# Expert rows added to h in memory by an accumulating scatter for each block, in the mixture-of-experts tail of a hybrid decoder step

## The reference, cut to what matters

```python
h = h + concat([attn_out, ssd_out]) @ w_out
h = h + hier_moe(rmsnorm(h, norm2_w), ...)      # top 2 of 8 experts inside the top 1 of 4 groups
y = rmsnorm(h, norm_f_w)

# hier_moe -> grouped_experts: each (token, k) pair goes to a slot of its expert,
# blocks of rows belong to one expert
hdn = silu(xb @ w_gate[e]) * (xb @ w_up[e])      # 1024 -> 512
yr = hdn @ w_down[e]                             # 512 -> 1024
out = zeros.at[row_tok].add(yr * row_w[:, None]) # row_w is the gate of that pair
```

## Time and profile before

| | us |
|---|---|
| median of 3 runs | 3809.22 |
| the profiled execution, its own time | 3812.94 |
| its span, first to last instruction | 3811.1 |
| all stages ahead of mix_out end at about | 2277.9 |
| last slot made (L2573) | 2640.6 |
| experts' first instruction | 2688.46 |
| first transpose of gathered rows | 2707.26 |
| last copy of an expert result ends | 3674.08 |
| first gather of combine | 3679.63 |

### The profile page before, as it was taken

The page is one execution under the profiler, slowest core; times in us unless marked ns, Lnnn a source line. Parts: engine busy times, 40 slices in busy tenths (PEclk is TensorE's granted clock), DMA queues, the critical chain, the costliest instruction groups (busy, mean ns, idle before and its releaser), DMA issues. The chain is left out here.

```text
span 3811.1 us, 44653 instructions
## 1 busy us (share of the span) xinstructions
PE 2979.4 (78%) x14961; PEld 1473.1 (39%) x14962; DVE 1582.6 (42%) x3644; ACT 1132.2 (30%) x2026; POOL 732.2 (19%) x858
## 2 busy tenths in 40 slices
PE   7998986982884575777775659995599999999950
PEld 3545352560442233545553434552133333333310
DVE  1154676856672278888663322333000000100025
ACT  1131452641441257985453220110011111111111
POOL 1403030300221142323233310002210001000124
PEclk9999998966775786898997779997799999999975
DMA  5010110001222210110003534330677667877757
GB/s 183 31 37 32 43 35 32 27 14 38 67 77 72 75 41 28 33 34 15 12 12 130 178 124 164 110 109 29 198 271 261 226 242 251 285 262 242 254 160 260
DMA packets 234028, 447.55 MB, mean 117 GB/s; under 512 B 49385, under 2 KB 86473, under 8 KB 233884
## 3 DMA queue, kind: packets, MB, share of 16 engines
q1 hardware_dynamic: 192988, 334.49, 25.9%
q0 software_dynamic: 27616, 89.49, 7.1%
q10 hardware_dynamic: 13280, 21.77, 1.8%
HBM read 359.98 MB, written 85.69 MB: 117 GB/s over the span
## 5 line engine op out<-in xcount | busy, mean ns | idle before, releaser
L759 PE MATMUL pj_cm<-pj_xT,pj_w 128*64 128x512 f32 (+3 forms) x1520 | 435.0, 549 | 6.5 <-DVE pj_xT L440 5.8
L2792 PE MATMUL ex_pgu<-ex_wgu,ex_xT 128*64 128x512 f32 x1344 | 297.7, 595 | 0.0
L2792 PE MATMUL ex_pgu<-pre_down_wgu,ex_xT 128*64 128x512 f32 x1312 | 292.5, 599 | 0.7 <-ACT ex_xT L2712 0.7
L759 PEld LDWEIGHTS pj_cm<-pj_xT,pj_w 128*64 128x64 f32 (+1 forms) x1520 | 192.0, 186 | 241.3 <-issue 230.4
L2757 DVE TENSOR_TENSOR ex_hid<-ex_sg,ex_pgu 128x256 f32<-128x256 f32 x83 | 34.9, 421 | 595.5 <-ACT ex_sg L2716 595.5
L1976 PE MATMUL ap_SB<-keep_kT,ap_qs 64*128 64x512 f32 (+3 forms) x640 | 173.2, 635 | 93.4 <-DVE ap_m L1908 79.5
L1987 PE MATMUL ap_TB<-keep_const,ap_L 128*128 128x128 f32 x1088 | 176.6, 306 | 68.6 <-ACT ap_PT L1769 47.8
L1757 ACT ACTIVATE ap_L<-ap_L,ap_nm 128x128 f32<-128x128 f32 (+15 forms) x128 | 153.2, 1197 | 178.9 <-DVE ap_nm L1913 168.2
L686 ACT ACTIVATE pj_U<-pj_sc,pj_cand 128x512 bf16<-128x512 f32 (+4 forms) x155 | 183.3, 1184 | 65.4 <-DVEq L521 65.2
L500 DVE TENSOR_SCALAR_CACHE_REDUCE pj_U<-pj_sc,pj_cand 128x384 bf16<-128x384 f32 (+9 forms) x182 | 194.8, 1103 | 14.2 <-issue 0.5
L1987 PEld LDWEIGHTS ap_TB<-keep_const,ap_L 128*128 128x128 f32 x1088 | 130.0, 153 | 149.8 <-ACT ap_L L1757 60.4
(11 more groups left out here) (502 smaller groups left out, 4859.1 us busy)
## 6 DMA issues: line engine op xcount, KB each, us to landing
pre_down_wgu<-in_w_gate SPq DMA_DIRECT2D x16, 2048.0 KB
pre_down_wgu<-in_w_up SPq DMA_DIRECT2D x16, 2048.0 KB
pre_down_wd<-in_w_down SPq DMA_DIRECT2D x16, 2048.0 KB, 8.9
ex_wgu<-in_w_gate SPq DMA_DIRECT2D x16, 2048.0 KB
ex_wgu<-in_w_up SPq DMA_DIRECT2D x16, 2048.0 KB
ex_wd<-in_w_down SPq DMA_DIRECT2D x16, 2048.0 KB
yslot<-ex_y ACTq DMA_DIRECT2D x166, 128.0 KB
pj_x<-in_x_prompt SPq DMA_DIRECT2D x16, 512.0 KB, 4.8
```

Source lines behind the costliest of these rows:

```text
L759: mm = pe.matmul(cm[u % 2][cols * n:cols * n + cols, 0:width_], w[:, k, c0:c0 + cols], xT[:, k, 0:width_], start=(k == 0), stop=(k == KD - 1))
L2792: mm = pe.matmul(pgu[BR * t:BR * t + BR, :], xT[:, k % 4, k // 4, :], wgu[par][:, k, :, 256 * t:256 * t + 256], start=(k == 0), stop=(k == ...
```

## The change

1. **mix_out, slot map.** The 34 scatters to `slot_tok`, its zeroing and its reading back are gone. In their place the map from slot to token and from slot to gate is a product on PE: slot = 64 x block + row; for each of the 34 (tile, k) columns a one-hot of the row (`onerow`, 64 wide) times a one-hot of the block, scaled once by (token - 2080) and once by the gate (`oneblk`, 2 x 98 wide), accumulated in one PSUM bank. From it DVE makes `rows` (source half rows), `dest` (half rows of `h` to add to; an empty slot goes to a spare row behind the tokens) and `gmap` (gate for each slot). Two small broadcast loads are added at the start, and DVE waits for them.
2. **experts.** DVE's copy of the result multiplies by the gate. ACT's two stores are gone. POOL adds the result to `h` in memory with one accumulating indirect DMA for each block; each waits until the one before has landed. POOL's order becomes gather(b+3), add_rows(b+1), gather(b+4), add_rows(b+2), ...
3. **combine** only normalises `h`: no gathers, no additions, four buffers in place of two, the stores issued by ACT, loads by SP.

```diff
# mix_out, sync
-            sp.wait_ge(sm["xn_ok"], 1)
-            sp.dma_start(io["slot_tok"].rearrange("(p b) o -> p (b o)", p=P), zeroi[:]).then_inc(sm["zero_st"], 16)
+            sp.dma_start(rowio[:], io["keyrow"][0:1, 0:BR].to_broadcast([P, BR])).then_inc(sm["io_in"], 16)
+            sp.dma_start(blkio[:], io["keyrow"][0:1, 0:MAXBLK].to_broadcast([P, MAXBLK])).then_inc(sm["io_in"], 16)
...
+            sp.dma_start(io["h"][TOK:TOK + BR, :], xr[0:BR, 0, :]).then_inc(sm["b_st"], 16)
# mix_out, gpsimd
-            for t in range(NT):
-                rows = P if t < TILES else DEC
-                for k in range(2):
-                    pool.indirect_dma_start(io["slot_tok"], bass.IndirectOffsetOnAxis(ap=keep["slot"][0:rows, 2 * t + k:2 * t + k + 1], axis=0),
-                                            toki[0:rows, t:t + 1], None).then_inc(sm["scat"], 16)
-            pool.wait_ge(sm["scat"], 16 * 2 * NT)
# mix_out, vector
             v.wait_ge(sm["w_in"], 16 * 5)
+            v.wait_ge(sm["io_in"], 32)
...
+            v.tensor_scalar(blki[:], keep["slot"][:], SHIFT, None, ALU.arith_shift_right)
+            v.tensor_scalar(ranki[:], keep["slot"][:], BR - 1, None, ALU.bitwise_and)
+            v.drain()
+            v.tensor_copy(blkf[:], blki[:])
+            v.tensor_copy(lowf[:], ranki[:])
+            v.tensor_scalar(tokm[:], keep["tok"], float(-TOK), None, ALU.add)
+            v.drain()
+            q = 2 * NT // 2
+            for c in range(2):
+                sl = slice(q * c, q * c + q)
+                v.tensor_tensor(onerow[:, sl, :], bc(rowio[:].unsqueeze(1), [P, q, BR]), bc(lowf[:, sl].unsqueeze(2), [P, q, BR]), ALU.is_equal)
+                for i in range(q * c, q * c + q):
+                    r = slice(0, rows_of(i // 2))
+                    v.tensor_scalar(oneblk[r, i, 0, :], blkio[r, :], blkf[r, i:i + 1], tokm[r, i // 2:i // 2 + 1], ALU.is_equal, ALU.mult)
+                    v.tensor_scalar(oneblk[r, i, 1, :], blkio[r, :], blkf[r, i:i + 1], keep["gate"][r, i // 2, i % 2:i % 2 + 1], ALU.is_equal, ALU.mult).then_inc(sm["oh_ok"], 1)
+            v.memset(keep["rows"][:, MAXBLK:MAXBLK + 2], 0)
+            v.wait_ge(sm["map_ok"], 1)
... four small operations on 64 x 98, then for both halves rows, dest and gmap
# mix_out, tensor
+            for i in range(2 * NT):
+                r = slice(0, rows_of(i // 2))
+                pe.wait_ge(sm["oh_ok"], i + 1)
+                mm = pe.matmul(pl[0:BR, 0:2 * MAXBLK], onerow[r, i, :], oneblk[r, i].rearrange("p n b -> p (n b)"), start=(i == 0), stop=(i == 2 * NT - 1))
+            mm.then_inc(sm["map_ok"], 1)
# experts, gpsimd
+            pool.sem_inc(sm["y_done"], 1)
+            n = pool.value_load(keep["blocks"][0:1, NEXP:NEXP + 1], min_val=NEXP, max_val=MAXBLK)
+
+            def gather(b):
                 pool.wait_ge(sm["turned"], b + 1)
                 pool.tensor_copy(cur[:], rows[:, ds(b, 1)])
                 pool.drain()
                 pool.indirect_dma_start(xg[:], None, halves, bass.IndirectOffsetOnAxis(ap=cur[:], axis=0)).then_inc(sm["xg_in"], 16)
+            def add_rows(b, begins=False):
+                if not begins:
+                    pool.wait_ge(sm["y_st"], b * 16)
+                    pool.sem_inc(sm["y_done"], 1)
+                pool.tensor_copy(to[:], keep["dest"][:, ds(b, 1)])
+                pool.drain()
+                pool.wait_ge(sm["y_cp"], b + 2)
+                pool.sem_inc(sm["go"], 1)
+                pool.indirect_dma_start(sums, bass.IndirectOffsetOnAxis(ap=to[:], axis=0), y[:], None, compute_op=ALU.add).then_inc(sm["y_st"], 16)
+
+            for b in range(3):
+                gather(b)
+            add_rows(0, True)
+            with pool.Fori(0, n - 1) as b:
+                gather(b + 3)
+                add_rows(b + 1)
+            pool.wait_ge(sm["y_st"], n * 16)
# experts, vector
-                v.wait_ge(sm["y_st"], 32 * b + 32)
-                v.tensor_copy(y[:], py[:]).then_inc(sm["y_cp"], 1)
+                v.wait_ge(sm["y_done"], b + 1)
+                v.tensor_scalar(y[:], py[:], keep["gmap"][:, ds(b, 1)], None, ALU.mult).then_inc(sm["y_cp"], 1)
# experts, scalar: store(b - 1) gone; experts, sync: the load of slot_tok and the zeros to unused blocks gone
# combine
+            for t in range(NB):            # NB = 4 buffers, loads on SP
+                load(t)
+            for t in range(NB, NT):
+                sp.wait_ge(o_ok, t - NB + 1)
+                load(t)
...
+            for t in range(NT):            # scalar: square and sum, and the store of the tile two before
+                r = slice(0, rows_of(t))
+                s.wait_ge(h_in[t % NB], 16 * (t // NB + 1))
+                if t >= NB:
+                    s.wait_ge(ms_ok, t - NB + 1)
+                s.activation(junk[r, :], h[r, t % NB, :], ACT.Square, accum_out=ssq[r, t % NB:t % NB + 1]).then_inc(sq_ok, 1)
                 s.drain()
+                if t >= 2:
+                    store(t - 2)
...
+            mean(0)                        # vector
+            for t in range(1, NT):
+                mean(t)
+                scale(t - 1)
+            scale(NT - 1)
```

More of the change, by code:

```diff
@@ L43 @@
 MAXBLK = 98
+SHIFT = BR.bit_length() - 1
 GROUP = 4
@@ L146 @@
 PICK, PK = picks()
+KEYROW = np.arange(MAXBLK, dtype=np.float32)[None, :].copy()
 SHIFTS = np.arange(BITS - 1, -1, -1)
@@ L2639, in experts @@
         wd = [keep["ew_d"], a.sb("wd", [P, DE // P, D])]
-        slots = a.sb("slots", [P, MAXBLK], I32)
-        rows = a.sb("rows", [P, MAXBLK + 1], I32)
+        rows = keep["rows"]
         cur = a.sb("cur", [P, 1], I32)
@@ L2721, in turned_hidden @@
                 s.activation(hT[:], ph[:, 0:2 * P].rearrange("p (k h t) -> p k h t", k=2, h=2), ACT.Copy).then_inc(sm["h_ok"], 1)
-            def store(b):
-                row = s.snap(b * BR)
-                s.wait_ge(sm["y_cp"], b + 2)
-                for half in range(2):
-                    s.dma_start(io["yslot"][ds(row, BR), 512 * half:512 * half + 512], y[BR * half:BR * half + BR, :]).then_inc(sm["y_st"], 16)
             rows_out(0)
@@ L2732, in first @@
                 gate(b)
-                if not begins:
-                    store(b - 1)
                 turned_hidden(b)
@@ L2738, in rest @@
                 gate(b)
-                store(b - 1)
                 turned_hidden(b)
             over_blocks(s, first, rest)
-            n = s.value_load(keep["blocks"][0:1, NEXP:NEXP + 1], min_val=1, max_val=MAXBLK)
-            store(n - 1)
-            s.wait_ge(sm["y_st"], n * 32 + 32)
-            s.sem_inc(sm["go"], 1)
         @block.vector
@@ L2750, in _ @@
             v.sem_inc(sm["y_cp"], 1)
-            v.memset(rows[:, MAXBLK:MAXBLK + 1], 0)
-            v.wait_ge(sm["slot_in"], 32)
-            v.tensor_scalar(rows[:, 0:MAXBLK], slots[:], 2.0, keep["p_mod"][:, 3:4], ALU.mult, ALU.add).then_inc(sm["rows_ok"], 1)
             def hidden(b):
@@ L2881, in _ @@
[L2881 to L2882 removed]
             for t in range(NT):
[L2884 removed]
+                r = slice(0, rows_of(t))
                 pool.wait_ge(ms_ok, t + 1)
[L2886 to L2888 removed]
+                pool.tensor_tensor(rstd[r, t % NB:t % NB + 1], ms[r, t % NB:t % NB + 1], keep["half"][r, 0:1], ALU.pow).then_inc(pow_ok, 1)
@@ L2890, in _, with store @@
         @block.scalar
         def _(s):
-            def tile(t, par, rows):
-                s.wait_ge(mixed, t + 1)
-                s.activation(junk[0:rows, :], h[0:rows, par, :], ACT.Square, accum_out=ssq[0:rows, :]).then_inc(sq_ok, 1)
-                s.drain()
-            with s.Fori(0, TILES // 2) as j:
-                for par in range(2):
-                    tile(2 * j + par, par, P)
-            tile(TILES, 0, DEC)
+            def store(t):
+                rows = rows_of(t)
+                s.wait_ge(o_ok, t + 1)
+                dst = io["y_prompt"][0, t * P:(t + 1) * P, :] if t < TILES else io["y_sample"].rearrange("b t d -> (b t) d")
+                s.dma_start(dst, o[0:rows, t % NB, :]).then_inc(st[t % NB], 16)
@@ L2920, in _, with mean, scale @@
-            with v.Fori(0, TILES // 2) as j:
-                for par in range(2):
-                    tile(2 * j + par, par, P)
-            tile(TILES, 0, DEC)
+            def mean(t):
+                r = slice(0, rows_of(t))
+                v.wait_ge(sq_ok, t + 1)
+                if t >= NB:
+                    v.wait_ge(pow_ok, t - NB + 1)
+                v.tensor_scalar(ms[r, t % NB:t % NB + 1], ssq[r, t % NB:t % NB + 1], 1.0 / D, EPS, ALU.mult, ALU.add).then_inc(ms_ok, 1)
+            def scale(t):
+                r = slice(0, rows_of(t))
+                v.wait_ge(pow_ok, t + 1)
+                if t >= NB:
+                    v.wait_ge(st[t % NB], 16 * (t // NB))
+                v.scalar_tensor_tensor(o[r, t % NB, :], h[r, t % NB, :], rstd[r, t % NB:t % NB + 1], nf[r, :], ALU.mult, ALU.mult).then_inc(o_ok, 1)
```

129 lines of the change are left out of this document (51 added, 78 removed).

## The result

The changed kernel takes 4342.57 us (median of 4 runs, 4339.74 to 4347.91), the kernel before on the same chip 3811.77 us (median of 4, 3804.01 to 3815.8): 1.1395 times as long, with a 95% interval of 1.1367 to 1.1423. The forecast was 3874 us and its range ended at 3985. The sign was right, the size was not: +531 us instead of +65.

What follows compares the result with a forecast made beforehand. PE was taken to bound the experts, and the chain through each tile's second gather to bound combine. From 3812.9 us, -92 outside the loop and +157 in it gave 3878, 3874 on the median's level; range 3728 to 3985.

Steps and rivals of the forecast that it cites:

- The step that failed: Loop over blocks, POOL's order: after the scatter's issue, 0.4 and 1.02 us to the gather's issue, at +7.8 us.
- rival 2: Loop over blocks: the accumulating scatter is slow, 2 us more a block, +166 us, total 4040; chance 0.15.
- The waits, without the drain: Loop over blocks: PE waits for late gathers, 60 blocks of 2.3 us and 23 of 0.3, 145 us.
- 12 had been put in for the clock: Loop over blocks: pauses of 3 us let PE's clock fall to its lower level for a while, +12 us.
- -14: Slot map in mix_out: 33 us in place of 47.8 from last slot to the experts' first instruction.
- -9.8: Start of the experts: 9.0 us in place of 18.8 from first instruction to first turn.
- my lower case: Slot map in mix_out: DVE as the slower side and PE at full clock, 25 us (-23).
- Combine: Last stage: 60 us in place of 131.5, at 3.0 us a tile with four buffers, -71.5 us.
- The start of mix_out: DVE's first sum waits for two small loads queued behind weights: +2 us, at least 0, at most 3.
- rival 3: Slot map and combine give less, -63 in place of -92: total 3903; chance 0.53 together with the forecast.
- Rival 1: Loop over blocks: gathers issued later land faster and the loop hides them, total 3717 without stalls; chance 0.26.
- the list of signs: Signs of another error: a result's copy waiting for the previous scatter, or a scatter's issue far above 1 us on POOL.

Runs made afterwards that it cites:

- e1: Changed kernel with both index copies and one drain ahead of the wait for the result, then scatter and gather with no drain between: 3947.11 us, 1.0382 of before.
- e9: The kernel with gather following scatter undrained, plus one POOL drain put back between the two: 4345.84 us, 1.1422 of before.
- e3: Changed kernel with a plain scatter that overwrites rows of h in place of adding, drains kept: 4138.61 us, 1.0886 of before.
- e7: Changed kernel with the gather issued before the scatter and both index copies and the only drain ahead of both: 3705.94 us, 0.9739 of before.
- e6: Changed kernel with the gather issued before the scatter, drains kept, and two buffers in combine in place of four: 3901.29 us, 1.0267 of before.

## Why the prediction was wrong, step by step

**The step that failed** is this one: "then 0.4 to the index copy, and 1.02 from that to the gather's issue". The 1.02 us came from the earlier trace rows, where it runs from the index copy at 2993.13 to the gather at 2994.15, and 0.33 us of it was a drain. I took the interval as the price of a fixed sequence. It was the price of that sequence with nothing of POOL's in flight, and the change puts exactly that drain behind a DMA. From the scatter's issue to the gather's passed 7.0 us in the block above, where the prediction had 1.4, and the drain in it took 4.8 us in the median. e1 against e9 puts some 396 us on the drain between the two.

**The rest of that step.** The scatter's issue took 1.60 us, not the 0.98 of a gather, and the scatter landed after 4.9 us (median), against 3.2 and 6.7 for a gather. The prediction held "2 us more in each block", +166 us, open as rival 2, with the gather's packets behind the scatter's in the queue. Without the drain that mechanism is there but small: e1's gathers in quiet blocks take 4.1 to 4.7 us in place of 3.5, and such blocks are 12.1 to 12.3 us long where nothing before them was late, not above 13. With the drains in place e3 puts some 200 us on the accumulation, of which 81 are the scatter's own. That this is near rival 2's +166 is chance. With the gather first and one drain (e7) the scatter's landing of 8.1 us cost nothing.

**The waits, without the drain, were about right.** e1 is the loop as the prediction saw it: PE waited 188.6 us there, 11.7 of them for the very first gather, so 177 against the forecast 145. By its timeline 48 blocks waited for 2.6 to 3.9 us, about 150 us together, where 60 blocks of 2.3 were forecast, and some 29 for less than a us, 0.55 in the mean, where 23 of 0.3 were: the landings beside weights are the mechanism that the prediction gave, with fewer blocks and longer waits. `down` was busy for 181.5 + 179.3 = 361 us in it, 58 over before, where 12 had been put in for the clock. That term was too small even here: in the changed kernel `down` took 5.35 us after a pause of 3.36, and the only pause in the rows I had read was 2.29 us.

**The clock in the changed kernel** cost 159 us (137 + 22) in place of 12, as nearly every block had a pause: in 76 of 80 blocks of the timelines `down` was longer than 3.65 us. By itself it is no cause: e7 has the same products at a granted clock of 1.00.

**Slot map and start.** "-14" and "-9.8" came to -34.7 together, 10.9 better. I had put the 34 products at half clock, 0.69 us each. 33 of their 68 records took 7.95 us, which is 0.24 us each and 0.48 a product: the pace of DVE, whose operations, two to a product, are 0.24 us apart. From the last slot to the experts' first instruction passed 2658.89 - 2634.51 = 24.4 us (33 forecast); my lower case, "DVE as the slower side and full clock 25 us", was the right one. From there to the first turn 7.5 us (9.0 forecast).

**Combine.** 58.9 us after, 60 forecast. The working held: e6 shows that it is the loop of a buffer that sets the pace, 6.0 us a tile with two buffers against 3.0 forecast with four.

**Sum of the parts outside the loop.** The start of mix_out took 1.8 us longer (from its first load, issued at 2266.89, to DVE's first sum at 2297.63, 30.7 us where it was 28.9), +2 forecast; the end of the experts came 3.9 us dearer, +1 forecast. With these, 1.8 - 34.7 - 72.6 + 3.9 = -102 us, forecast -92. e7, whose loop runs at PE's pace, is 98 us faster by the medians. Its trace has 3811.1 - 3704.2 = 106.9 us less, but its last slot comes 7.1 us earlier than in the trace before, and in the changed kernel's trace mix_out itself begins 9.6 us earlier: stages that the change leaves alone vary by this much from one execution to another. Two figures of the prediction do not follow from its own terms. The slot map is 47.8 - 33 = 14.8, not 14; and the ends of its parts add up to -110 and -73, not "-115 and -63", so that rival 3 would be 3893 and not 3903. Neither changes the forecast's side.

Rival 1 ("the loop hides them", 3717) is near the time that e7 reached, 3706, by an order of POOL's work that the change did not have. Its reason, that gathers issued later land faster, is borne out where they came latest: behind the changed kernel's gathers the drain took 3.48 us in the median, and the one at 3217.63 was used 3.5 us after its issue. At +16.3 that no longer helped; in e1, at +7.9, the one shown took 7.1.

**What the list of signs had.** It named "a scatter whose issue takes far more than 1 us on POOL" as what would make the forecast wrong; 1.60 was more, and not the main thing. A copy of the result that waits for the scatter before it, its other sign, showed once (6.6 us). It did not name POOL itself waiting.

The Trainium skill, "DMA: Bandwidth & Descriptors", section on the anatomy of one DMA, has a fit by which a gather of 256 KB lands after an estimated 2.6 us. This case's traces agree only roughly in quiet stretches and not beside the weights: the gather's drains in the changed kernel took 3.14 us at the shortest, 3.48 in the median and 7.45 at the longest, and in e1 the gather shown took 7.1 us.

## What to carry to other kernels

A duration read for a short sequence of instructions holds for the state the engine was in; before it is moved, ask what will be in flight there, and above all what a drain in it will find. On POOL, make all index tiles and drain once while nothing of the engine's is in flight, then issue the DMAs, the one that another engine waits for first. A stall on TensorE costs more than its length, so a forecast of waits needs the price of the next products at the lower clock beside it.

## What the runs showed of the hardware that I had not expected

- A drain on POOL waits for POOL's indirect DMAs in flight: 0.25 to 0.46 us with none, in the median 3.5 us behind a gather, 4.8 to 5.2 behind an accumulating scatter and 6.05 behind the plain one of e3, of which more fell beside weight loads; 8.7 at the longest. Only the drain does: an indirect DMA was issued 0.31 us behind another in flight.
- An indirect DMA that adds takes 1.60 us to issue, a plain scatter of the same 256 KB 0.99, the gather 1.01. It landed after 4.6 us at the shortest, the plain one after 2.7; in the median after 4.9 us in the changed kernel, and after 7.8 and 8.1 in e1 and e7, where a gather was in flight beside it.
- PE's granted clock: after pauses of 3.4 to 3.6 us a `down` of 16 records took 5.35 us in place of 3.65 in most blocks of the changed kernel, but in e1 one came through at 3.65 after 3.36 us. What tells these cases apart was not found.
